# Expert weights of a mixture-of-experts block in 2 MB pair transfers, 16 KB in one piece for each partition

## What is computed

```
def moe_ffn(h, w_router, b_router, w_gate_up, b_gate_up, w_down, b_down):
    logits = (x2 @ w_router).astype(jnp.float32) + b_router.astype(jnp.float32)
    top_val, top_idx = lax.top_k(logits, TOP_K)
    gate = jax.nn.softmax(top_val, axis=-1)
    ...
        gu = xb @ w_gate_up[e] + b_gate_up[e]
        gt = jnp.minimum(gu[:, :D_FF], SWIGLU_LIMIT)
        up = jnp.clip(gu[:, D_FF:], -SWIGLU_LIMIT, SWIGLU_LIMIT)
        glu = gt * jax.nn.sigmoid(gt * SWIGLU_ALPHA)
        return ((up + 1.0) * glu) @ w_down[e] + b_down[e]
```

## Time and profile before

| | us |
|---|---|
| median of 3 runs | 1377.14 |
| lowest, highest run | 1375.26, 1377.79 |
| the profiled execution's own time | 1372.17 |
| its span, first to last instruction | 1370.3 |
| TensorE busy (matmul) | 1326.4 |
| of it L1401, 2048 matmuls | 475.3 |
| of it L1435, 1024 matmuls | 234.4 |
| DMA, mean over the span | 364 GB/s |

### The profile page before, as it was taken

How to read it: one execution, slowest core, us unless ns; L and a number is a source line. 1 busy time by engine, 2 the same in 40 slices (tenths; PEclk the granted TensorE clock), 3 DMA queues, 4 the chain that set the end, 5 groups by cost and what they waited for, 6 DMA issues and landing times.

```text
span 1370.3 us, 15645 instructions
## 1 busy us (share of the span) xinstructions
PE 1326.4 (97%) x6572; PEld 531.8 (39%) x6572; DVE 415.1 (30%) x785; ACT 198.9 (15%) x425; POOL 26.5 (2%) x40
## 2 busy tenths in 40 slices
PE   7999998999999999999999999999999999999995
PEld 3446676677543333333333333333333333332321
DVE  3232443223533322222232222232222222222234
ACT  2211424322111010001010000001000101000002
POOL 0000003300000000000000000000000000000000
PEclk9999999999999999999999999999999999999998
DMA  6686484789989999999999999999999999999994
GB/s 250 246 319 265 155 312 169 239 247 338 338 339 385 394 416 417 418 417 418 417 417 416 416 418 417 419 417 417 417 416 417 417 417 419 417 417 416 416 393 159
DMA packets 114794, 498.69 MB, mean 364 GB/s; under 512 B 8816, under 2 KB 31984, under 8 KB 81296
## 3 DMA queue, kind: packets, MB, share of 16 engines
q1 hardware_dynamic: 113872, 495.15, 91.2%
q0 software_dynamic: 848, 2.49, 0.5%
HBM read 495.15 MB, written 36.96 MB: 388 GB/s over the span
## 4 chain that ended last, share of the span: by engine, by line
PE 89%; DMA 7%; DVE 2%; ACT 1%; issue 1%; SPq 1%; DVEq 0%
PE ps L1401 30%; PE ps L1435 15%; PE ps L994 7%; PE ps L1388 7%; PE ps L1345 6%; PE ps L969 5%; DMA ring<-in_w_gate_up 3%; PE ps L1235 2%; PE ps L1227 2%; DMA ring<-in_w_down 2%; PE ps L1109 2%; PE ps L1355 1%; PE ps L1093 1%; PE ps L1422 1%; PE ps L1029 1%; PE ps L978 1%
## 5 line engine op out<-in xcount | busy, mean ns | idle before, releaser
L1401 PE MATMUL ps<-ring,cring 128*64 128x512 f32 x2048 | 475.3, 601 | 1.5 <-DVE cring L1785 1.2
L1401 PEld LDWEIGHTS ps<-ring,cring 128*64 128x64 f32 x2048 | 136.4, 137 | 298.2 <-issue 277.7
L1435 PE MATMUL ps<-ring,cring 128*64 128x512 f32 x1024 | 234.4, 599 | 2.4 <-DMA ring<-in_w_down 1.3
L1880 DVE TENSOR_TENSOR x_tok<-x_tok,ps 128x1024 f32<-128x1024 f32 (+1 forms) x99 | 120.3, 1217 | 372.4 <-PE ps L1388 372.4
L1435 PEld LDWEIGHTS ps<-ring,cring 128*64 128x64 f32 x1024 | 67.9, 136 | 142.9 <-issue 140.0
L1388 PE MATMUL ps<-cring 64*128 64x512 f32 (+1 forms) x384 | 105.5, 627 | 0.7 <-issue 0.7
L994 PE MATMUL ps<-hT,ring 128*128 128x288 f32 x384 | 100.5, 419 | 0.0
L1785 DVE TENSOR_TENSOR cring<-ps,params 128x512 f32<-128x512 f32 x32 | 22.1, 692 | 247.0 <-PE ps L1355 247.0
L874 ACT ACTIVATE cring<-ps 128x512 f32<-128x512 f32 x32 | 19.1, 597 | 507.3 <-PE ps L1422 507.3
L1345 PE MATMUL ps<-h_tok,cring 128*64 128x512 f32 x372 | 91.2, 607 | 0.0
L994 PEld LDWEIGHTS ps<-hT,ring 128*128 128x128 f32 x384 | 73.2, 194 | 25.5 <-issue 6.6
(11 more groups left out here) (304 smaller groups left out, 822.2 us busy)
## 6 DMA issues: line engine op xcount, KB each, us to landing
ring<-in_w_gate_up SPq DMA_DIRECT2D x256, 1024.0 KB, 18.1
ring<-in_w_down SPq DMA_DIRECT2D x128, 1024.0 KB, 17.0
ring<-in_w_in SPq DMA_DIRECT2D x10, 2048.0 KB, 7.8
out_dil_k_s<-in_cache_dil_k SPq DMA_DIRECT2D x8, 2044.0 KB
out_dil_v_s<-in_cache_dil_v SPq DMA_DIRECT2D x8, 2044.0 KB
cring<-in_cache_dil_k SPq DMA_DIRECT2D x8, 512.0 KB, 3.9
ring<-in_w_out SPq DMA_DIRECT2D x2, 2048.0 KB, 11.5
cring<-in_cache_dil_k SPq DMA_DIRECT2D x24, 128.0 KB, 4.1
```

The lines of the kernel that those rows point to most:

```text
L1401: ins = pe.matmul(bank(gu0 + u)[64 * h:64 * h + 64, :], xTe[:, k % 4, (k // 4) * 64:(k // 4) * 64 + 64], ring[:, a:a + 512], start=(k == 0 ...
L1435: ins = pe.matmul(bank(5)[64 * h:64 * h + 64, :], aTe[:, kk % 4, (kk // 4) * 64:(kk // 4) * 64 + 64], ring[:, a:a + 512], start=(kk == 0), ...
L1880: v.tensor_tensor(x_v[0:r, t, :], x_v[0:r, t, :], bank(at, 2)[0:r, :], ALU.add).then_inc(S["sc_added"], 1)
```

## The change

A transfer is now a pair of slots, 2 MB, with 16 KB in one piece for each partition: six a block in place of twelve, with six semaphores. Pair k < 4 takes 256 rows of w_gate_up, and partition p gets rows 2p and 2p + 1 of them, which lie side by side in HBM. Pairs 4 and 5 take 512 rows of w_down each, and partition p gets rows 4p to 4p + 3. SP issues a pair when both slots have been used; TensorE waits once for each pair. As a slot then holds the weights of features 256k + 2p + c (gate-up) or 512j + 4p + c (down), the transposes read every 2nd column of `xg_sb`, and every 4th of `act`, so that each partition gets its features. The gains of the norm are laid out anew in the parameters for that, 8 more columns.

```
-        slice_in = [sem(f"slice{k}_in") for k in range(12)]
+        pair_in = [sem(f"pair{k}_in") for k in range(6)]
...
-            def load_slice(k, e):
-
-                dst = ring[:, k * SLOT:(k + 1) * SLOT]
-                if k < 8:
-                    src = d["w_gate_up"][0, e, k * P:(k + 1) * P, :]
+            def load_pair(k, e):
+
+                if k < 4:
+                    src = d["w_gate_up"][0, e, 256 * k:256 * (k + 1), :].rearrange("(p c) n -> p (c n)", c=2)
                 else:
-                    src = d["w_down"][0, e, (k - 8) * 2 * P:(k - 7) * 2 * P, :].rearrange("(c p) n -> p c n", p=P)
-                    dst = dst.rearrange("p (c n) -> p c n", c=2)
-                return sp.dma_start(dst, src)
+                    src = d["w_down"][0, e, 512 * (k - 4):512 * (k - 3), :].rearrange("(p c) n -> p (c n)", c=4)
+                return sp.dma_start(ring[:, 2 * k * SLOT:2 * (k + 1) * SLOT], src).then_inc(pair_in[k], 16)
...
             for i in W_BR:
                 wait_wblk_used(sp, i)
-                for k in (2 * (i - 12), 2 * (i - 12) + 1):
-                    load_slice(k, 0).then_inc(slice_in[k], 16)
+                load_pair(i - 12, 0)
             sp.wait_ge(S["merged"], 8)
-            for k in range(8, 12):
-                load_slice(k, 0).then_inc(slice_in[k], 16)
+            load_pair(4, 0)
+            load_pair(5, 0)
...
             def load_gate_up(b):
-                for k in range(8):
-                    sp.wait_ge(S["gu_used"], 8 * (b - 1) + k + 1)
-                    load_slice(k, b).then_inc(slice_in[k], 16)
+                for k in range(4):
+                    sp.wait_ge(S["gu_used"], 8 * (b - 1) + 2 * k + 2)
+                    load_pair(k, b)
 
             def load_down(b):
-                for k in range(8, 11):
-                    sp.wait_ge(S["d_used"], 3 * (b - 1) + k - 7)
-                    load_slice(k, b).then_inc(slice_in[k], 16)
+                sp.wait_ge(S["d_used"], 3 * (b - 1) + 2)
+                load_pair(4, b)
                 sp.wait_ge(S["y_done"], b)
-                load_slice(11, b).then_inc(slice_in[11], 16)
+                load_pair(5, b)
...
                 for q in range(4):
-                    ins = pe.transpose(bank(7)[:, q * P:(q + 1) * P], xg_sb[:, q * P:(q + 1) * P], ident)
+                    rows = xg_sb[:, 256 * (q // 2):256 * (q // 2) + 256].rearrange("p (f c) -> p c f", c=2)[:, q % 2, :]
+                    ins = pe.transpose(bank(7)[:, q * P:(q + 1) * P], rows, ident)
...
                 for k in range(KC):
-                    pe.wait_ge(slice_in[k], 16 * b + 16)
+                    if k % 2 == 0:
+                        pe.wait_ge(pair_in[k // 2], 16 * b + 16)
...
-                    ins = pe.transpose(bank(4)[:, q * P:(q + 1) * P], act[:, q * P:(q + 1) * P], ident)
+                    ins = pe.transpose(bank(4)[:, q * P:(q + 1) * P],
+                                       act.rearrange("p (f c) -> p c f", c=4)[:, q, :], ident)
...
-                    pe.wait_ge(slice_in[8 + j], 16 * b + 16)
+                    if j % 2 == 0:
+                        pe.wait_ge(pair_in[4 + j // 2], 16 * b + 16)
...
-            gain_x = gain_v[:, 2, :].rearrange("p (h q) -> p q h", h=2).unsqueeze(3).to_broadcast([P, 4, 2, BT])
+            gain_x = gain_pair.rearrange("p (h q) -> p q h", h=2).unsqueeze(3).to_broadcast([P, 4, 2, BT])
```

More of the change, by code:

```diff
@@ L116, in lay_params @@
         np.broadcast_to(b_router.reshape(1, NE), (P, NE)),
-        w_router.reshape(KC, P, NE).transpose(1, 0, 2).reshape(P, KC * NE)], 1), dtype=np.float32)
-NPARAM = 3 * KC + 8 + 2 + NE + KC * NE
+        w_router.reshape(KC, P, NE).transpose(1, 0, 2).reshape(P, KC * NE),
+        gain_rows[2].reshape(4, P, 2).transpose(1, 0, 2).reshape(P, KC)], 1), dtype=np.float32)
+NPARAM = 3 * KC + 8 + 2 + NE + KC * NE + KC
 CONST_AT = constants()[1]
@@ L190, in build @@
         b_rt = params[:, 34:34 + NE]
-        wrt_v = params[:, 34 + NE:NPARAM].rearrange("p (k e) -> p k e", e=NE)
+        wrt_v = params[:, 34 + NE:34 + NE + KC * NE].rearrange("p (k e) -> p k e", e=NE)
+        gain_pair = params[:, NPARAM - KC:NPARAM]
         bias_raw = [pT[:, 512 * i:512 * (i + 1)] for i in (0, 1)]
@@ L548, in _ @@
                 wait_wblk_used(sp, i)
-                for k in (2 * (i - 12), 2 * (i - 12) + 1):
-                    load_slice(k, 0).then_inc(slice_in[k], 16)
+                load_pair(i - 12, 0)
             sp.wait_ge(S["merged"], 8)
-            for k in range(8, 12):
-                load_slice(k, 0).then_inc(slice_in[k], 16)
+            load_pair(4, 0)
+            load_pair(5, 0)
             for n in range(2):
                 sp.wait_ge(S["wout_done"], 5 + n)
-                for k in (4 + 2 * n, 5 + 2 * n):
-                    load_slice(k, 0).then_inc(slice_in[k], 16)
+                load_pair(2 + n, 0)
@@ L559, in load_dyn @@
             def load_dyn(k, e):
-                dst = ring[:, k * SLOT:(k + 1) * SLOT]
-                if k < 8:
-                    src = d["w_gate_up"][0][bass.ds(e, 1), k * P:(k + 1) * P, :].rearrange("o p n -> (o p) n")
-                else:
[L564 to L567, removed]
+                if k < 4:
+                    src = d["w_gate_up"][0][bass.ds(e, 1), 256 * k:256 * (k + 1), :].rearrange("o (p c) n -> (o p) (c n)", c=2)
+                else:
+                    src = d["w_down"][0][bass.ds(e, 1), 512 * (k - 4):512 * (k - 3), :] \
+                        .rearrange("o (p c) n -> (o p) (c n)", c=4)
@@ L594, in _ @@
                         sp.wait_ge(S["gu_used"], 8 * b)
-                        for k in range(8):
-                            load_dyn(k, e).then_inc(slice_in[k], 16)
+                        for k in range(4):
+                            load_dyn(k, e)
                         sp.wait_ge(S["y_done"], b)
-                        for k in range(8, 12):
-                            load_dyn(k, e).then_inc(slice_in[k], 16)
+                        for k in range(4, 6):
+                            load_dyn(k, e)
             y_p = d["y_p"][0].rearrange("(t p) n -> p t n", p=P)
```

## The result

| | before | after |
|---|---|---|
| median, us (9 runs each) | 1377.14 | 1384.30 |
| lowest, highest | 1371.66, 1377.98 | 1380.59, 1387.69 |
| the profiled execution's own time | 1372.17 | 1385.42 |
| its span | 1370.3 | 1383.4 |
| mean granted clock over the span | 0.991 | 0.984 |

The ratio after to before is 1.0059, 95% interval [1.0043, 1.0075]: some 7 us slower where I forecast no change. It lies inside my range of 1371 to 1386 only because that was widened for rivals B and C.

What follows compares the result with a forecast made beforehand. TensorE was taken to set the pace for 27 blocks, DMA only at the end. Weight waits saved 2.9 us and the last pair cost 2.3: -0.6 us, 1371.6 profiled, 1376.5 us as median, range 1371 to 1386.

Steps and rivals of the forecast that it cites:

- Rival B: Strided weight loads slow TensorE in every block, in L1422: 1380 to 1394.5 us, slower; chance 0.22.
- Rival C: 16 KB pieces move no faster, so the DMA deficit stays 0.54 us per block: 1383 us, slower; chance 0.08.
- the stalls of 1.59 us go: Blocks near the end: TensorE's 1.59 us lateness from weight waits, part of 2.9 us in all, vanishes with faster transfers.
- One of my signs: DMA over the blocks: its share falls under 1 while the rate rises to 425 GB/s, if the forecast is right.
- A 16 KB piece in 0.597 us: DMA weight transfers: piece time extrapolated from 4 and 8 KB pieces, making a block 28.2 us, below TensorE's 29.63.
- Transposes. I take nothing: Stepped stationary reads in L1355 and L1422: forecast cost nothing, with bounds of nothing and 36 us for both lines.
- rival B's mild form: L1422: only the first load of each group shows, 32 x 0.14 = 4.5 us, giving 1381 us.
- The row of L1109: Matmul whose moving operand jumps 64 bytes after four values yet takes 273 ns; cited for stepped reads costing nothing.
- The last pair is waited for, 2.3 us: Last stage: expert 31's w_down pair 4 lands at 1340.9 us, while down(31) could start at 1338.6, adding 2.3 us.
- Pair 5 was in time: Last stage: expert 31's second w_down pair lands near 1345.8 us, wanted at 1346.7, so it holds by 1 us.
- Rival A: Unprofiled runs wait some 5 us more for weights than the profile, all of which would go: 1371.5 us; chance 0.32.
- a median much nearer the profile: Whole kernel after the change: sign that the extra weight waits of unprofiled runs, 5 us, had existed and gone.

Runs made afterwards that it cites:

- a1: Changed kernel with all transposes reading neighbouring columns again, features unmatched to weights; median 1376.94 us, ratio to the kernel before 1.0009.
- a3: Changed kernel with the permutation moved from TensorE's reads to ScalarE's and VectorE's writes; median 1377.94 us, ratio to the kernel before 1.0015.
- a4: Changed kernel's 2 MB pairs with the old row layout (8 KB and 4 KB pieces) and transposes without a step; median 1383.90 us, ratio 1.0063.
- c0: The changed kernel itself measured once more; median 1381.45 us, ratio to the kernel before 1.0043.
- c1: Changed kernel with act written permuted by VectorE, only the xg_sb transposes keeping their 8-byte step; one execution, 1374.88 us, block period 29.71 us.
- c2: Changed kernel with xg_sb written permuted by ScalarE, only the act transposes keeping their 16-byte step; one execution, 1383.28 us, block period 29.71 us.
- d0: Repeat of the changed kernel with the permutation in ScalarE's and VectorE's writes instead of TensorE's reads; median 1378.04 us, ratio to the kernel before 1.0016.
- b4: Kernel before, in 1 MB slices, with expert 31's w_down loaded early into freed slots; median 1376.41 us, ratio to the kernel before 1.0008.

## Why the prediction was wrong

- **TensorE sets the pace, the stalls of 1.59 us go: right.** No L1398 waits for weights, landings stay at medians of 10.4 to 11.3 us. One of my signs did not come: the DMA share stayed at 1.00, since it does not tell a queue that keeps up from one that limits.
- **A 16 KB piece in 0.597 us: somewhat too small.** It took 0.612 at the fastest seen, between my value and my bound of 0.622. It decided nothing: 29.4 us by the bound still stays under TensorE's 29.63.
- **"Transposes. I take nothing": this is the step that failed.** It measured 69 ns a load, 0.086 us a group, 0.173 a block, 5.2 us in all, between my bounds of 0 and 36. It turned "no change" into slower. My reason was that a load of 140 ns lies beside matmuls of 273 ns. But the records of matmuls overlap: in the kernel before, the starts of the four matmuls in a group of L1422 are 165, 109 and 109 ns apart (medians of 32 groups), so a record of 273 ns does not mean 273 ns of cover. With loads of 209 ns (L1419) they are 223, 120 and 120 ns apart. The first distance is most of the cost (58 of 86 ns), as rival B's mild form had it, but in both lines, not only L1422; the others take 11 ns each. The row of L1109, my other reason, has its step in the moving operand, and no run here sets the two operands side by side.
- **The last pair is waited for, 2.3 us: right mechanism, size too small.** From down(30) to down(31) I had 10.95 us; it took 11.40. The first pair landed 7.58 us after its issue where I had 7.3, and down(31) began 0.14 us behind the landing. And I left out the clock's fall that came with the wait: 1.56 us. Together this term gives 1.4 + 1.6 = 3.0 over the kernel before, where mine gave 2.3 - 1.32 = 1.0. Pair 5 was in time: no second wait stands in down(31).
- **Rival A fell.** a1 and a3 have no wait for weights in any block before the end, and their medians are not 5 us lower but 0.8 and 1.8 higher. What lies between profile and median fits the clock ahead of the experts. My sign for A, "a median much nearer the profile", could not have told the two apart.
- **Rival B happened**, at its mild end: 1376.5 + 5.2 + 2.0 for the end = 1383.7; measured 1384.3. The time alone would fit rival C (1383) as well; the period of 29.80 us and the flat landings tell them apart.
- **Rival C** did not, but a4 shows what it would have been: 5.6 us forecast, 7.8 measured by the medians and 6.6 by the profiles; the clock's fall was missing here too.

The chances were too even: C and B together had 0.30, and a new kind of read on the engine that sets the pace in every block, with no row that shows it, deserved more than 0.22.

## What to carry to other kernels

Where one engine is busy for a whole period, anything that lengthens its instruction counts, and "hidden beside the matmul" has to be read from the distance between starts, not from the length of records. Put a permutation into the write of an engine that has idle time: here 840 ns a block on ScalarE and VectorE cost nothing, and 173 ns a block on TensorE cost 5 us in all. Before moving a load forward, find out which transfer is awaited and when it was issued. A larger transfer is wanted for its pieces; its size delays both the issue and the first use, and the place to look for that is the last stage, where nothing is left to cover it.

## What I had not expected of the hardware

- A weight load of 128 x 128 f32 for a transpose takes 140 ns from neighbouring columns and 209 ns with a step of 8 or of 16 bytes; I saw no difference between the steps.
- A wait of 3.24 us on TensorE came with 3.4 us at half clock (0.52 in that stretch). So did the same wait, 3.3 to 3.6 us, in the profiles of a1, a3, a4, c0, c1, c2 and d0 (in c0 6.8 us); the fall began between 1.3 us before the wait's end and 0.9 behind it. The waits of 1.32 and 1.37 us in the kernel before and in b4 were not.
- Writing neighbouring values 128 columns apart lengthens a 128x512 operation from 597 to 1074 ns on ScalarE and from 692 to 1054 ns on VectorE.
- The DMA share was 1.00 both at 423 and at 425 GB/s, in streams that kept up with the demand.
